# A two-layer decoder trunk on Trainium2: the residual kept transposed, the norm's root applied at eviction, expert down rows read four to a partition

## The chip, the cores and the metric

The kernel runs on one core of a Trainium2 chip. The metric is the time of the whole program on the device, in microseconds. PE is the matrix engine, DVE the vector engine, ACT the scalar engine, POOL the GpSimd engine, SP the queue that issues most of the transfers.

## What is computed

256 tokens of 1,024 features, float32 throughout, go through two layers and a last norm. Each layer adds a mixer and then a mixture of experts to the residual `h`:

```python
for layer in range(DEPTH):                       # DEPTH = 2
    hn = rms_norm(h, attn_norm_g[layer])         # x * rsqrt(mean(x^2) + eps) * gain
    if layer % 2 == 0: mix = mixer_ab(hn, ...)   # stick-breaking and retention heads
    else:              mix = mixer_c(hn, ...)    # windowed attention, with biases
    h = h + mix
    h = h + hierarchical_moe(rms_norm(h, ffn_norm_g[layer]), ...)
return rms_norm(h, final_norm_g)
```

The experts: 32 of them in 4 groups. A token takes the best group and the two best experts in it. An expert is `(silu(x @ w_gate[e]) * (x @ w_up[e])) @ w_down[e]`, with w_gate and w_up 1024x512 and w_down 512x1024. All weights of all experts are read once a layer: 32 x 3 matrices of 2.097 MB.

## The kernel before

**Weights.** A unit is one 2 MB block of weights, 16 KB on each partition. SP loads units into seven ring slots and four spare ones of the `arena` (the expert loop goes round over eight of these; three more, parked, hold down units of the first quad). A slot is reloaded when PE has counted up `used` for what was in it. Gate and up units are read as eight consecutive rows to a partition, one run of 16 KB; a down unit with `a (m p) n -> p (a m) n` (line 355), four rows of 4 KB that lie 128 rows apart.

**Residual and norms.** `h` lies with tokens on partitions, two blocks of 128. A norm (numbered 0 to 4: before mixer 0, experts 0, mixer 1, experts 1, and the last) does, for each block: ACT squares with a sum (`mean_squares`, 538), POOL adds eps and raises to -1/2 (`inverse_rms`, 473), DVE scales into `hr` (`norm`, 1138), PE turns eight tiles (`turn_normed`, 693), DVE evicts them times the gain into `hnT`, features on partitions (`spread_normed`, 1148). Only then can PE project (`project`, 717, and `in_proj`, 730).

**Mixer 0.** Seven input units; the first two go out transposed, products of 256 moving columns, the rest with 512 (lines 743 and 720). ACT evicts them (`evac`, 553). Heads are worked between the units. `out_proj` (846) takes token blocks as the stationary side and 512 weight columns as the moving one, in a low part (heads of the first kind) and a high part (second kind), and block 1's last products are broken by the turning of block 0's norm. `residual` (1244) adds two banks of a block to `h`.

**Experts** (PE 884, DVE 1259, ACT 600, POOL 486, SP 370). Router logits come out transposed from normed rows (`logits_of`, 703), go through ACT and are turned (`turn_logits`, 712). DVE chooses in some 20 small steps (1271 to 1293), PE ranks, DVE makes a 0/1 matrix `pick`. A quad is four experts with 32 token slots each. For quad i PE gathers its tokens (`gather`, 899: products of `hr` and `pick`), DVE evicts them times the gain (`take_rows`, 1334), `four` (907) does gate, up and down with four experts side by side, and `combine` (934) multiplies the output by the weighted pick into token rows, summed over all quads in four banks. After the first products of a quad have freed slots, SP issues the next loads, so that the transfers run ahead of PE. There are eight quads a layer.

**Mixer 1** adds its input bias at eviction (`add_bias`, 1392); POOL adds the output bias to `h` during the attention (521). `out_low` (1070) fills PE's waits between heads. After experts 1, the last norm is written block by block and sent out (453 to 457).

## Time and profile before

| | us |
|---|---|
| three runs: median, lowest, highest | 1250.41, 1247.34, 1256.53 |
| the profiled execution, and the span in it | 1254.63, 1252.8 |
| PE busy, DVE busy, ACT busy, POOL busy | 837.8, 174.4, 117.8, 44.2 |
| mean granted clock of PE, as a share of full | 0.832 |

The page cuts the span into 40 equal slices of 31.3 us and gives the share of each engine in tenths for each. The other views are the chain of work that ended last, the timeline of instructions, groups of instructions by line, and windows, which add up busy time, granted clock and transfer rate between two times. Times are microseconds from the span's start. "x128" counts instruction records; a float32 product has two of them. In brackets at the end of a timeline row stand the idle time before it and what ended it.

### The profile page before, as it was taken

To read this page: it belongs to the slowest core of one execution; us is meant where nothing else is said; L and a number is where in the kernel's file an instruction comes from. 1 tells how busy PE (TensorE), PEld (TensorE's weight loads), DVE (VectorE), ACT (ScalarE), POOL (GpSimd) and SP (SyncE) were. 2 spreads that over 40 slices of the span, in tenths; PEclk is the share of its full clock that TensorE was granted. 3 is DMA by queue.
4 is the path that set the end of the run, shared out by engine and by line. 5 is a ranking of instruction groups with operands and counts; after the bars stand their busy time and mean duration, and the time that the engine had idled before them with its cause. 6 is when DMAs were issued, how large, how long until landed. Compare 5 with 4: busy or idle time off the path is not lost.

```text
span 1252.8 us, 11735 instructions
## 1 busy us (share of the span) xinstructions
PE 837.8 (67%) x4938; PEld 382.0 (30%) x4938; DVE 174.4 (14%) x404; ACT 117.8 (9%) x237; POOL 44.2 (4%) x55
## 2 busy tenths in 40 slices
PE   6999978473737465565669898856473737465565
PEld 5655444131303121212224574512131303121211
DVE  1042432000000000000023543300000000000001
ACT  1145110000000000000010321000000000000001
POOL 0010100000000000000001300000000000000000
PEclk9999989787879696977779788887786879697868
DMA  9932744999999999999995435399999999999992
GB/s 368 385 135 96 275 195 195 422 417 428 418 424 423 423 422 421 429 418 428 416 403 213 177 135 201 134 428 419 429 416 424 422 423 421 423 427 420 426 417 120
DMA packets 66362, 439.00 MB, mean 350 GB/s; under 512 B 3601, under 2 KB 3601, under 8 KB 49809
## 3 DMA queue, kind: packets, MB, share of 16 engines
q1 hardware_dynamic: 65888, 435.97, 85.0%
q10 hardware_dynamic: 432, 2.43, 0.5%
q8 instruction: 32, 0.52, 0.2%
q14 instruction: 10, 0.07, 0.0%
HBM read 437.34 MB, written 1.05 MB: 350 GB/s over the span
## 4 chain that ended last, share of the span: by engine, by line
DMA 48%; PE 40%; SPq 6%; DVE 3%; issue 1%; ACT 1%; POOL 1%; POOLq 0%; DVEq 0%; ACTq 0%
PE bank L923 18%; DMA arena<-in_w_gate 17%; DMA arena<-in_w_down 15%; DMA arena<-in_w_up 14%; PE bank L720 9%; SPq L361 6%; PE bank L850 4%; PE bank L743 2%; PE bank L691 2%; DMA ring<-in_w_in_ab 1%; PE bank L903 1%; PE bank L708 1%; DVE h L1247 1%; PE bank L775 0%; PE bank L940 0%
## 5 line engine op out<-in xcount | busy, mean ns | idle before, releaser
L923 PE MATMUL bank<-ring,hnT 128*32 128x512 f32 x1792 | 283.6, 716 | 298.1 <-DMA ring<-in_w_up 82.0
L923 PEld LDWEIGHTS bank<-ring,hnT 128*32 128x32 f32 x1792 | 74.3, 129 | 486.1 <-issue 369.2
L923 PE MATMUL bank<-ring,arena 128*32 128x512 f32 x800 | 131.4, 683 | 61.0 <-DMA arena<-in_w_down 37.7
L923 PE MATMUL bank<-arena,hnT 128*32 128x512 f32 x256 | 142.9, 722 | 0.0
L720 PE MATMUL bank<-ring,hnT 128*128 128x512 f32 x256 | 114.4, 603 | 1.7 <-DVE hnT L1151 1.7
L1344 DVE TENSOR_TENSOR arena<-arena,bank 128x512 f32<-128x512 f32 x16 | 11.0, 688 | 565.8 <-PE bank L923 565.8
L923 PE MATMUL bank<-arena 128*32 128x512 f32 x224 | 78.8, 634 | 2.0 <-ACT arena L619 2.0
L923 PEld LDWEIGHTS bank<-ring,arena 128*32 128x32 f32 x800 | 36.6, 123 | 142.2 <-issue 123.5
L903 PE MATMUL bank<-arena,hr 128*128 128x128 f32 x512 | 65.5, 289 | 2.0 <-DVE arena L1311 2.0
L720 PEld LDWEIGHTS bank<-ring,hnT 128*128 128x128 f32 x256 | 48.4, 193 | 59.8 <-issue 56.9
L903 PEld LDWEIGHTS bank<-arena,hr 128*128 128x128 f32 x512 | 62.4, 203 | 14.0 <-issue 11.7
L940 PE MATMUL bank<-hnT,arena 128*128 128x512 f32 x128 | 57.7, 594 | 1.5 <-issue 1.5
L850 PE MATMUL bank<-ring,arena 128*128 128x512 f32 x128 | 57.8, 598 | 0.6 <-ACT arena L681 0.3
L619 ACT ACTIVATE arena<-bank 128x512 f32<-128x512 f32 x16 | 9.6, 597 | 339.3 <-PE bank L691 339.3
L490 POOL TENSOR_TENSOR arena<-arena,gate_all 128x256 f32<-128x256 f32 x16 | 9.9, 616 | 806.8 <-PE bank L691 772.6
L615 ACT ACTIVATE arena<-bank 128x512 f32<-128x512 f32 x16 | 9.6, 597 | 304.6 <-PE bank L923 304.6
L691 PE MATMUL bank<-early,arena 128*128 128x128 f32 x216 | 36.7, 301 | 2.2 <-DVE arena L1344 1.8
L1348 DVE COPY hnT<-bank 128x512 f32<-128x512 f32 x16 | 11.1, 691 | 178.2 <-PE bank L923 178.2
L691 PEld LDWEIGHTS bank<-early,arena 128*128 128x128 f32 x216 | 26.9, 153 | 25.6 <-issue 22.0
L923 PEld LDWEIGHTS bank<-arena,hnT 128*32 128x32 f32 x256 | 31.8, 129 | 9.6 <-issue 9.6
L850 PEld LDWEIGHTS bank<-ring,arena 128*128 128x128 f32 x128 | 23.3, 190 | 26.1 <-issue 26.1
L940 PEld LDWEIGHTS bank<-hnT,arena 128*128 128x128 f32 x128 | 23.1, 190 | 26.2 <-issue 26.2
(159 smaller groups left out, 532.2 us busy)
## 6 DMA issues: line engine op xcount, KB each, us to landing
ring<-in_w_gate SPq DMA_DIRECT2D x56, 2048.0 KB, 20.8
ring<-in_w_up SPq DMA_DIRECT2D x56, 2048.0 KB, 21.7
ring<-in_w_down SPq DMA_DIRECT2D x50, 2048.0 KB, 20.4
arena<-in_w_down SPq DMA_DIRECT2D x14, 2048.0 KB, 23.1
arena<-in_w_up SPq DMA_DIRECT2D x8, 2048.0 KB, 29.7
arena<-in_w_gate SPq DMA_DIRECT2D x8, 2048.0 KB, 28.9
ring<-in_w_in_ab SPq DMA_DIRECT2D x7, 2048.0 KB, 21.2
ring<-in_w_in_c SPq DMA_DIRECT2D x3, 2048.0 KB, 20.2
```

The lines of the kernel that those rows point to most:

```text
L361: sp.dma_start(view(j, LOOP_SLOTS[l][k]), expert_unit(l, e, j // QUAD)).then_inc(moe[l]["landed"][k], 16)
L691: return pe.transpose(dst, src, ident)
L708: op = pe.matmul(bank[2 * b][0:ROUTER, 0:P], router[:, l, k, :], hnT[:, k, b * P:(b + 1) * P], start=(k == 0), stop=(k == KD - 1))
L720: op = pe.matmul(dst[b][:], hnT[:, k, b * P:(b + 1) * P], unit[:, k, :], start=(k == 0), stop=(k == KD - 1))
L743: op = pe.matmul(dst[c // 2][:, (c % 2) * S:(c % 2 + 1) * S], slot_in(s)[:, k, c * P:(c + 1) * P], hnT[:, k, :], start=(k == 0), stop=(k = ...
L850: op = pe.matmul(bank[banks[2 * b + half]][:], t[:, c, b * P:(b + 1) * P], unit[:, c % 4, half * HALF:(half + 1) * HALF], start=(c == 0), ...
L903: op = pe.matmul(of_block(bank[4 + k // 4], k % 4), hr[:, b, k, :], pick[:, b, :], start=(b == 0), stop=(b == NB - 1))
L923: op = pe.matmul(dst[rows, :], lhsT[:, q, rows], unit[s][:, q, cols], start=(q == 0), stop=(q == steps - 1))
L940: op = pe.matmul(bank[2 * b + half][:], pick_wT[:, b * P:(b + 1) * P], e_y[:, half * HALF:(half + 1) * HALF], start=first, stop=last, skip ...
L1247: op = dve.tensor_tensor(h[:, b, cols], h[:, b, cols], bank[banks[2 * b + half]][:], ALU.add)
L1344: dve.tensor_tensor(e_h, e_h, bank[7][:], ALU.mult).then_inc(m["hidden"], 1)
L1348: dve.tensor_copy(e_y[:, 0:HALF], bank[4][:]).then_inc(m["y_low"], 1)
```

## The change

- The residual is `hT`, features on partitions, in eight chunks of 128 features (feature p*8+k in chunk k). The input comes transposed and the output leaves so; the host turns both and reorders the columns of the two output projections.
- Output projections and `combine` put out such chunks: weights or expert output are the stationary side, 256 tokens the moving one. DVE adds a chunk as soon as it is done, ACT multiplies it by the norm's gain into `hg` (`scale_chunk`) and squares it (`square_chunk`). DVE or POOL sum the squares of the chunks, PE sums over partitions, POOL takes the root.
- Projections work on `hg`, without the root. The root is put in at eviction: by ACT as a scale, in `add_bias`, in the rotary tables, or, for the two transposed units, as a row spread over the partitions by PE from a diagonal. Router logits stay without it (the choice doesn't change; the two exponentials take it as a scale).
- For the gather, PE turns 16 tiles of `hg` and ACT evicts them times the root (`tokens_out`). The rows of a quad carry the gain already; DVE and ACT evict one half each.
- Down units are read as four consecutive rows to a partition. PE turns the hidden rows with a step of four, and DVE and ACT evict the output with a step of eight.
- The output bias comes with the late table and is added in `residual`; the last gain is a column in the gain table. Their two row loads go. ACT issues its four table loads at once. The first weight unit and the input come in two halves each, alternating.

```diff
+hT = sb("hT", [P, KD, S])
+hg = sb("hg", [P, KD, S])
 hr = sb("hr", [P, NB, KD, P])
-hnT = sb("hnT", [P, KD, S])
+sq_sum = sb("sq_sum", [P, S])
+gains = sb("gains", [P, NORMS, KD])
...
-return w_down[l, one].rearrange("a (m p) n -> p (a m) n", p=P)
+return w_down[l, one].rearrange("a (p m) n -> p (a m) n", m=MH)
...
-for b in range(NB):
-    sp.dma_start(h[:, b, :], x_v[:, b, :]).then_inc(x_in[b], 16)
-for u in range(AB_UNITS):
+for j in range(2):
+    ks = slice(4 * j, 4 * j + 4)
+    sp.dma_start(hT[:, ks, :], xT[:, ks, :]).then_inc(x_in[j], 16)
+    sp.dma_start(slot_in(0)[:, ks, :], w_ab_v[:, ks, 0:HALF]).then_inc((first_half_in, w_landed[0])[j], 16)
+for u in range(1, AB_UNITS):
...
-last = experts(0, [(sinks_b[:], sinks, SWA_HEADS), (c_bin, b_in_c, C_IN * HALF), (c_bout, b_out_c, D)])
+last = experts(0, [(sinks_b[:], sinks, SWA_HEADS), (c_bin, b_in_c, C_IN * HALF)])
...
-experts(1, [(final_gain, final_norm_g, D)])
-for b in range(NB):
-    sp.wait_ge(out_ready, b + 1)
-    sp.dma_start(out_v[:, b, :], hr[:, b].rearrange("p k c -> p (k c)")).then_inc(out_done, 16)
-sp.wait_ge(out_done, 16 * NB)
+experts(1, [])
...
+    pool.wait_ge(ms_out, n + 1)
+    pool.tensor_tensor(rstd[:, n, :], ms[:, n, :], minus_half[:, 0:NB], ALU.pow).then_inc(rooted, 1)
+
+def sum_squares(n):
+    for k in range(1, KD):
+        pool.wait_ge(squares, KD * n + k + 1)
+        op = pool.tensor_tensor(sq_sum[:], sq_sum[:] if k > 1 else squared[:, 0, :], squared[:, k, :], ALU.add)
+        if k < KD - 1:
+            link(op)
+    op.then_inc(summed, 1)
...
+act.dma_start(gains[:].rearrange("p n k -> p (n k)"), gain_table).then_inc(gains_in, 16)
 act.dma_start(early[:], early_table).then_inc(early_in, 16)
...
+def scale_chunk(n, k):
+    act.activation(hg[:, k, :], hT[:, k, :], ACT.Copy, scale=gains[:, n, k:k + 1]).then_inc(scaled, 1)
+
+def square_chunk(n, k):
+    act.activation(squared[:, k, :], hT[:, k, :], ACT.Square, scale=D ** -0.5).then_inc(squares, 1)
+
+def wait_chunk(n, k):
+    act.wait_ge(h_done, KD * (n - 1) + k + 1)
+
+act.wait_ge(gains_in, 16)
+for k in range(KD):
+    if k % 4 == 0:
+        act.wait_ge(x_in[k // 4], 16)
+    scale_chunk(0, k)
+    if k % 4 == 3:
+        for j in range(k - 3, k + 1):
+            square_chunk(0, j)
+
+def tokens_out(l):
+
+    n = 2 * l + 1
+    act.wait_ge(ms_done, n + 1)
+    act.activation(ms[:, n, :], bank[OUT_BANKS[l][1]][:, SUMS:SUMS + NB], ACT.Copy,
+                   bias=EPS).then_inc(ms_out, 1)
+    act.wait_ge(rooted, n + 1)
+    for high in range(2):
+        for b in range(NB):
+            act.wait_ge(hr_turned, 4 * l + 2 * high + b + 1)
+            op = act.activation(flat(hr[:, b, 4 * high:4 * high + 4, :]), hr_bank(l, b, high)[:], ACT.Copy,
+                                scale=rstd[:, n, b:b + 1])
+    op.then_inc(hr_done, 1)
...
+for k in range(KD):
+    wait_chunk(2 * l + 1, k)
+    scale_chunk(2 * l + 1, k)
+    square_chunk(2 * l + 1, k)
+tokens_out(l)
...
-act.activation(e_y[:, HALF:D], bank[5][:], ACT.Copy).then_inc(m["y_high"], 1)
+act.activation(e_y[:, :, CAP * 2:P], by_partition(bank[5]), ACT.Copy).then_inc(m["y_high"], 1)
...
+def take_high(i):
+    act.wait_ge(m["gathered"], i + 1)
+    act.activation(flat(xeT[:, 4:8, :]), bank[5][:], ACT.Copy).then_inc(m["xe_high"], 1)
...
+for k in range(KD):
+    if u == 0 and k == 4:
+        mean_squares(0, bank[4])
+        pe.wait_ge(w_landed[s], 16)
+    if u == 0:
+        pe.wait_ge(scaled, k + 1)
+    for c in range(4):
         op = pe.matmul(dst[c // 2][:, (c % 2) * S:(c % 2 + 1) * S],
-                       slot_in(s)[:, k, c * P:(c + 1) * P], hnT[:, k, :],
-                       start=(k == 0), stop=(k == KD - 1))
+                       slot_in(s)[:, k, c * P:(c + 1) * P], hg[:, k, :],
+                       start=(k == 0 and c % 2 == 0), stop=(k == KD - 1), skip_group_check=True)
...
+def out_proj(l, t, unit, part, steps=range(32), order=range(KD)):
     for step in steps:
-        half, c = step // 4, 4 * part + step % 4
-        op = pe.matmul(bank[banks[2 * b + half]][:], t[:, c, b * P:(b + 1) * P],
-                       unit[:, c % 4, half * HALF:(half + 1) * HALF], start=(c == 0), stop=(c == KD - 1))
+        k, c = order[step // 4], step % 4
+        op = pe.matmul(chunk_of(OUT_BANKS[l], k), unit[:, c, k * P:(k + 1) * P], t[:, 4 * part + c, :],
+                       start=(part == 0 and c == 0 and k < 4), stop=(part == 1 and c == 3),
+                       skip_group_check=True)
     return op
+
+def logits_of(l, k):
+    pe.wait_ge(scaled, KD * (2 * l + 1) + k + 1)
+    if k == 0:
+        pe.wait_ge(late_in, 16)
+    for b in range(NB):
+        lo = b * LOGIT_PITCH
+        op = pe.matmul(bank[FREE_BANKS[l][0]][:, lo:lo + ROUTER], hg[:, k, b * P:(b + 1) * P],
+                       router[:, l, k, :], start=(k == 0 and b == 0), stop=(k == KD - 1),
+                       skip_group_check=True)
+    if k == KD - 1:
+        op.then_inc(moe[l]["logits"], 1)
+
+def turn_rows(l, high):
+    for b in range(NB):
+        for k in range(4):
+            op = turn(of_block(hr_bank(l, b, high), k), hg[:, 4 * high + k, b * P:(b + 1) * P])
+        op.then_inc(hr_turned, 1)
+
+def out_proj_high(l, t, unit, done):
+    for k in range(KD):
+        if k >= 4:
+            pe.wait_ge(h_done, KD * 2 * l + k - 3)
+        op = out_proj(l, t, unit, 1, range(4 * k, 4 * k + 4))
+        op.then_inc(done, 1)
+        if k > 0:
+            logits_of(l, k - 1)
+    logits_of(l, KD - 1)
+    turn_rows(l, 0)
+    mean_squares(2 * l + 1, bank[OUT_BANKS[l][1]])
+    turn_rows(l, 1)
...
+out_proj(0, catT, slot_out(0), 0, range(2 * pair, 2 * pair + 2))
...
+out_proj(0, catT, slot_out(0), 0, range(8, 28))
 for b in range(NB):
     pe.wait_ge(ab["gn"], b + 1)
     for c in range(4):
         op = turn(of_block(bank[2 + b], c), r_c[:, b, c * P:(c + 1) * P])
     op.then_inc(ab["gn_turned"], 1)
+out_proj(0, catT, slot_out(0), 0, range(28, 32)).then_inc(ab["used"], 1)
 pe.wait_ge(w_landed[(AB_IN + 1) % RING], 32)
-pe.wait_ge(ab["gn_cat"], 1)
-out_proj(catT, OUT_BANKS, 0, slot_out(1), 1).then_inc(ab["out"], 1)
 pe.wait_ge(ab["gn_cat"], 2)
-out_proj(catT, OUT_BANKS, 1, slot_out(1), 1, range(0, 6))
-turn_normed(1, 0)
-out_proj(catT, OUT_BANKS, 1, slot_out(1), 1, range(6, 8)).then_inc(ab["used"], 1)
+out_proj_high(0, catT, slot_out(1), ab["out"])
...
-for half in range(2):
-    for b in range(NB):
-        op = pe.matmul(bank[2 * b + half][:], pick_wT[:, b * P:(b + 1) * P],
-                       e_y[:, half * HALF:(half + 1) * HALF], start=first, stop=last,
-                       skip_group_check=True)
-        if last and half:
-            op.then_inc(m["combined"], 1)
+for k in range(KD):
+    if last and k >= 4:
+        pe.wait_ge(h_done, KD * (2 * l + 1) + k - 3)
+    op = pe.matmul(chunk_of(Y_BANKS, k), e_y[:, k, :], pick_wT, start=first and k < 4,
+                   stop=last, skip_group_check=True)
+    if last:
+        op.then_inc(m["combined"], 1)
...
-op = turn(of_block(bank[6], mh), e_h[:, mh * P:(mh + 1) * P])
+op = turn(of_block(bank[6], mh), e_h.rearrange("t (p m) -> t m p", m=MH)[:, mh, :])
...
+for step in range(NB * KD):
+    if step < KD:
+        pe.wait_ge(scaled, KD * 2 + step + 1)
+    if step == KD:
+        mean_squares(2, bank[5])
+    op = project([bank[j] for j in C_IN_BANKS[0]], slot_in(c_slot(0)), range(step, step + 1))
...
-pe.wait_ge(cc["att_low"], 1)
-out_low(0, 2)
 turn_low(1)
 turn_p(7)
-out_low(2, 5)
+pe.wait_ge(cc["att_low"], 2)
+out_low(0, 8)
 swa_values(6)
-out_low(5, 8)
+out_low(8, 16)
 swa_values(7)
-out_proj(attT, C_OUT_BANKS, 1, slot_out(c_slot(3)), 0).then_inc(cc["used"], 1)
+out_low(16, 32).then_inc(cc["used"], 1)
...
+mean_squares(4, bank[4])
+spread_rms(4, bank[5])
...
+for u, dst, by in ((0, sb_qT, over_rms_q), (1, sb_kT, over_rms)):
+    dve.wait_ge(ab["used"], u + 1)
+    for j in range(2):
+        op = dve.tensor_tensor(dst[:, 2 * j:2 * j + 2, :], bank[2 * u + j][:].rearrange("p (c n) -> p c n", c=2),
+                               by.unsqueeze(1).broadcast_to([P, 2, S]), ALU.mult)
+    op.then_inc(ab["qk_evac"], 1)
...
+def residual(k, banks, bias=False):
+    if bias:
+        op = dve.scalar_tensor_tensor(out=hT[:, k, :], in0=chunk_of(banks, k), scalar=out_bias[:, k:k + 1],
+                                      in1=hT[:, k, :], op0=ALU.add, op1=ALU.add)
+    else:
+        op = dve.tensor_tensor(hT[:, k, :], hT[:, k, :], chunk_of(banks, k), ALU.add)
     op.then_inc(h_done, 1)
-dve.wait_ge(ab["out"], 1)
-residual(0, OUT_BANKS)
-norm(1, 0)
-spread_normed(1, 0)
-dve.wait_ge(ab["used"], AB_UNITS)
-residual(1, OUT_BANKS)
-norm(1, 1)
-spread_normed(1, 1)
+def mixer_out(l, done):
+    for k in range(KD):
+        dve.wait_ge(done, k + 1)
+        residual(k, OUT_BANKS[l], bias=l == 1)
...
+mean_out(4, bank[4])
+rms_diagonal(4)
+dve.wait_ge(spread_done, 2)
+dve.wait_ge(scaled, NORMS * KD)
+by = bank[5][:, 0:S].unsqueeze(1).broadcast_to([P, 2, S])
+for j in range(KD // 2):
+    ks = slice(2 * j, 2 * j + 2)
+    dve.tensor_tensor(outT[:, ks, :], hg[:, ks, :], by, ALU.mult).then_inc(out_ready, 1)
```

## Rows read from the trace of the kernel before

**Rows 1.** The page, slices of 31.3 us: transfers in tenths, rate, and all packets.

```profile
DMA  9932744999999999999995435399999999999992
GB/s 368 385 135 96 275 195 195 422 417 428 418 424 423 423 422 421 429 418 428 416 403 213 177 135 201 134 428 419 429 416 424 422 423 421 423 427 420 426 417 120
DMA packets 66362, 439.00 MB, mean 350 GB/s; under 512 B 3601, under 2 KB 3601, under 8 KB 49809
```

**Rows 2.** The chain that ended last, in order of time: start, duration, what.

```profile
14.80 29.61 PE bank L743 x128
44.41 13.73 PE bank L720 x32
...
325.84 29.50 DMA arena<-in_w_gate
...
370.66 24.34 DMA arena<-in_w_down
```

**Rows 3.** Windows: length; busy (records) of PE, PEld, DVE, ACT, POOL; clock, DMA share, GB/s.

```profile
335.00:365.00 30.00, 18.16 (x130) 5.05 (x130) 1.12 (x2) 1.20 (x3) 0.61 (x1) 0.77 1.00 428
372.00:388.00 16.00, 13.05 (x95) 5.82 (x96) 0.69 (x1) 0.00 (x0) 0.00 (x0) 0.75 1.02 407
171.00:183.00 12.00, 8.08 (x43) 6.33 (x42) 3.98 (x5) 1.88 (x5) 0.79 (x2) 0.72 0.48 175
700.00:731.00 31.00, 27.43 (x135) 21.72 (x134) 20.39 (x65) 10.88 (x47) 9.06 (x4) 0.63 0.37 136
```

**Rows 4.** Timeline of the start: start, duration, engine, line, operation, tiles.

```profile
5.49 1.06 ACT L545 ACTIVATE hr<-h 128x1024 f32<-128x1024 f32 x1 [3.04 <-DMA h<-in_x]
```

**Rows 5.** Timeline, from mixer 0 to experts 0.

```profile
171.22 1.28 DVE L1247 TENSOR_TENSOR h<-h,bank 128x512 f32<-128x512 f32 x2 [0.87 <-PE bank L850]
...
183.09 0.17 DVE L1271 TENSOR_REDUCE tmp<-bank 128x2 f32<-128x8 f32 x1 [4.34 <-PE bank L714]
...
189.33 5.30 PE L903 MATMUL bank<-arena,hr 128*128 128x128 f32 x32 [1.00 <-DVE arena L1311]
...
196.01 7.07 PE L923 MATMUL bank<-ring,hnT 128*32 128x512 f32 x64 [1.27 <-DVE hnT L1337]
```

**Rows 6.** Timeline, from experts 0 to mixer 1.

```profile
642.47 3.67 PE L940 MATMUL bank<-hnT,arena 128*128 128x512 f32 x8 [0.76 <-issue]
...
652.97 8.93 PE L720 MATMUL bank<-ring,hnT 128*128 128x512 f32 x16 [0.78 <-DVE hnT L1151]
...
670.97 1.29 DVE L1397 TENSOR_TENSOR arena<-bank,arena 128x512 f32<-128x512 f32 x2 [7.21 <-PE bank L720]
```

**Rows 7.** Timeline, from mixer 1 to experts 1.

```profile
747.02 7.08 PE L850 MATMUL bank<-ring,arena 128*128 128x512 f32 x16
...
781.49 0.17 DVE L1271 TENSOR_REDUCE tmp<-bank 128x2 f32<-128x8 f32 x1 [4.40 <-PE bank L714]
...
787.72 6.42 PE L903 MATMUL bank<-arena,hr 128*128 128x128 f32 x32 [1.01 <-DVE arena L1311]
```

**Rows 8.** Timeline of the end.

```profile
1239.97 3.67 PE L940 MATMUL bank<-hnT,arena 128*128 128x512 f32 x8 [0.76 <-issue]
...
1248.42 1.28 DVE L1145 SCALAR_TENSOR_TENSOR hr<-h,rstd,arena 128x1024 f32<-128x1024 f32 x1 [0.77 <-POOL rstd L477]
```

**Rows 9.** Timeline inside experts 0, PE alone.

```profile
384.51 3.84 PE L903 MATMUL bank<-arena,hr 128*128 128x128 f32 x32
...
388.62 3.60 PE L940 MATMUL bank<-hnT,arena 128*128 128x512 f32 x8
```

**Rows 10.** Groups by line: form, count, busy and mean of one, idle time before.

```profile
L1141 DVE TENSOR_SCALAR hr<-h,rstd 128x1024 f32<-128x1024 f32 x8 | 10.7, 1333 | 18.1 <-POOL rstd L477 18.1
...
L490 POOL TENSOR_TENSOR arena<-arena,gate_all 128x256 f32<-128x256 f32 x16 | 9.9, 616 | 806.8 <-PE bank L691 772.6 <-DVE gate_all L1331 34.2
...
L627 ACT ACTIVATE arena<-bank 128x256 f32<-128x256 f32 x16 | 6.1, 378 | 6.1 <-PE bank L691 6.1
...
L1416 DVE TENSOR_TENSOR arena<-arena 128x256 f32<-128x256 f32 x4 | 1.4, 418 | 0.0
```

411 lines of the change are left out of this document (207 added, 204 removed).

## The prediction

> **What bounds the kernel now.** I read the page first, its slices and packets [rows 1]. Two long plateaus, the 8th to the 21st slice and the 27th to the 39th, have the DMA engines at 9 tenths and 403 to 429 GB/s: these are the two expert stages. Between them stand the mixers, with DMA at 2 to 7 tenths in the slices that they fill. So the kernel has two regimes. In an expert stage the end is set by bytes over rate; in a mixer, and in the hand-offs at its two ends, by the chain through PE and the small engines.
>
> The chain in order of time confirms it [rows 2]. The fourth load of a group of gates, issued at 325.84, lands 29.50 us later; that is the whole wait for the group. Four units of 2.097 MB at 428 GB/s are 19.6 us, so 9.9 us of older loads were still queued: PE may be that late before the DMA engines run dry. The windows show the rate [rows 3]: 428 GB/s while gate and up units land, 407 while down units land. The DMA share is full in both, so the difference is in how long the engines take for the same bytes.
>
> The same view has the first projection, and PE at full clock in it [rows 2]. Then I read the timeline at each hand-off: the start [rows 4], mixer 0 to experts 0 [rows 5], experts 0 to mixer 1 [rows 6], mixer 1 to experts 1 [rows 7], the end [rows 8]. There PE stands while squares, root, norm, 16 transposes and their evictions follow one another. From the last output product of mixer 0 (the next add starts at 171.22) to the first gate product at 196.01 are 24.8 us, in which DMA does little.
>
> **Prices.** A PE record (a product is two) is one pass. With 256 moving columns 128 records take 29.61 us, 0.231 each; with 512, 32 take 13.73 us, 0.429 [rows 2]. The gather's 32 records of 128 columns take 3.84 us inside a stage, 0.12 each [rows 9]; records with fewer columns I price the same. An ACT step of 128x256 is 0.38 us, a DVE step of 128x256 0.42, POOL's 0.62 [rows 10]; ACT's eviction of 128x512 is 0.60. For a hop between engines I put 0.07 us, a guess; a few hundredths more or less move no part by half a microsecond.
>
> **1. The start.** Before, PE's first projection starts at 14.80, released by the whole first unit [rows 2]. After, it needs the first half of x and of that unit. But ACT's queue no longer waits for the squares: early, late and decay tables (2.4 MB) are issued at once, ahead of the second x half in time. x had landed for the first square at 5.49 [rows 4]; the half unit (1.05 MB) plus the late table (0.5 MB) at 385 GB/s are 4.1 us more, so PE starts near 9.5 and its 64 records take 7.4, cold perhaps 9. The second half of x (0.5 MB) shares with decay (1.57 MB), 5.4 us, to about 14.5; then PE's sum of squares, placed ahead of k = 4, waits for 4 scalings, 4 squares and an add, 3.5 us, to 18.1. The remaining unit half lands near then too. Then 7.4 + 14.8 us and the spread of the root (1 us) end at 41.5 where 44.41 stood [rows 2]. I take 2.5 gained, with 0 (the tables take all of it) and 6 (no sharing) as bounds. Eviction of the first two units goes from ACT to DVE, with 7 adds, 2 copies and 4 table products; between 15 and 45 us DVE does nothing before, and PE's third unit covers it (14 us).
>
> **2. Mixer 0 to experts.** The output product is turned round: 64 products of 256 columns for 32 of 512, 128 x 0.231 = 29.6 us for 64 x 0.429 = 27.5, so 2 us more. Before, the last one ends at 171.2 [rows 5]. After, the high part can't start before both group norm blocks are turned; chunk 7 of the low part (1.85 us) covers this, so it starts near 157.7. Eight chunks of 1.85 us and seven logits of 4 records x 0.12 = 0.48 us give 18.2: the last chunk ends at 175.9. Behind it: add 0.42, scaling 0.38, logits 0.48, hops 0.2, together 1.4: the router starts at 177.3, where DVE's first router step stood at 183.09 [rows 5]. All other chunks' adds, scalings and squares lie under PE's 2.3 us a chunk, POOL's adds too (0.62). From there to the gather 6.24 us as before, to 183.5. In parallel runs what now feeds the gather: last square and POOL's add (1.9 us after the last chunk), 16 turned tiles and PE's sum of squares (to 3.8), ACT's copy, the root (0.57), ACT's four evictions of 0.6: 7.3 us after the chunk, 183.2. It just fits, so any slip there costs one for one. The gather took 5.30 us here and 3.84 inside the stage [rows 5, 9]; PE now idles less before it. The rows' eviction is split between DVE and ACT: 0.7 for 1.3. First gate product at 188.2 to 189.7 for 196.01: I take 7.0, bounds 3 and 9.
>
> A rule of the Trainium skill speaks against the warm gather: "TensorE: Matmul & The Clock Gate", section "Part 4: PE-mode transpose", says transposes don't count as PE work for the clock. Here the stretch 171 to 183, with turned rows in it, has a granted clock of 0.72 [rows 3]; no row shows whether they kept it low. By that rule both gathers stay cold and the sum is 3 us smaller.
>
> **3. The expert stages.** A down unit is now one run of 16 KB a partition, where it was four of 4 KB: 64 x 512 = 32,768 of the 49,809 packets under 8 KB are down's [rows 1]. It becomes the shape of a gate unit exactly, so I give it a gate unit's rate: 2.097 MB at 407 GB/s is 5.15 us, at 428 4.90, 0.25 less; a stretch in between would narrow it, so 0.24. 29 down units land in a saturated stage (the first quad's fourth and 28 more): 7.0 us. Bounds: 0 (the rate isn't from the run length) and 8. Each stage also read one row of 1,024 floats (output bias, final gain) to all 128 partitions, 0.5 MB, which now comes with a table or as 40 numbers a partition: 1.2 us each. So 8.1 a stage, 16.2 in all. PE's own work barely changes (combine: 16 records of 0.231 for 8 of 0.429, +0.3); DVE gives ACT half of the rows' eviction. In the quad shown combine ends at 392.2 and the down units land at 395.0 [rows 2, 9].
>
> **4. Experts 0 to mixer 1.** Before, combine starts at 642.47, the first projection at 652.97, and its bias is added at 670.97 [rows 6]. After, the 8 combine products take 3.7 us; adds (0.42) and scalings (0.38) follow at PE's 0.46 a chunk, and the waits from chunk 4 on are met. PE goes on at 646.2 with scaled chunks, 32 x 0.429 = 13.7 and 0.5 for the sum of squares: 660.5. Squares, adds and root are done about 8 us after the combine's start. Its weights landed long before. Saved 10.4, bounds 8 and 11.5.
>
> **5. Mixer 1 to experts 1.** The low output products now wait for both turned halves and have twice the records: their end at 754.1 [rows 7] becomes 755.9. The high part waits for both evictions, near 757.5. 18.2 us and 1.4 give the router at 777.1 for 781.49 [rows 7]; the gather, 6.42 us here, is 3.84 warm; the eviction saves 0.6. 5.0 to 7.6, I take 6.3.
>
> **6. The end.** Combine starts at 1239.97, the last scaling at 1248.42, span end 1252.8 [rows 8]: 12.8 us. After: ACT has 16 steps of 128x256 instead of two of 1.06 us: at 0.33 each (their starts overlap) 5.3 from 1.0 on, so 6.4; last add, PE's sum, mean, root, two diagonals and PE's spread 2.7; four DVE products of 0.69, 2.7; output DMA and the end as before, 3.1. 14.9: 2.1 lost, bounds 0 and 4.
>
> **Sum.** 2.5 + 7.0 + 16.2 + 10.4 + 6.3 - 2.1 = 40.3 us. The profiled execution took 1254.6 (span 1252.8), 4.2 above the median of the runs, 1250.4. I subtract from the median: 1210.
>
> **Strided reads.** Down's new row order makes PE turn the hidden rows with a step of four elements, and both copies of a quad's output read PSUM with a step of eight. No row shows either, for PE or for PSUM. In SBUF a step costs nothing: the norm that writes permuted took 1.33 us, the last, contiguous one 1.28 [rows 8, 10]. I take nothing. "SBUF — State Buffer" of the Trainium skill, section "Door 1: The DMA port swizzle", says that PSUM is read in lines of 8 bytes and steps beyond them cost; were the copies twice as long, only the last of each stage shows, 1.2 us in all.
>
> **Rivals.** (a) Down units keep 407 GB/s, because their rate comes from something else than the run length (their place in SBUF, PE's reads meanwhile). For it: the three kinds are loaded in turn, never alone. Against it: same bytes, same slots, same queue. Time 1210 + 14 = 1224. (b) The hand-offs give little: the sums of squares sit in PE's queue and ACT's evictions come after the root, so the gather waits in both layers. With 7 us of slip each, parts 2 and 5 are gone: 1210 + 13 = 1223; with a start that gains nothing, 1226. (c) The clock of mixer 1: 31 us at 0.63 [rows 3] shift in time; at full clock at most 31 x 0.37 = 11 us less, and about 8 with DVE and ACT on the same chain, or as much more if the next stretch falls too: 1202 to 1218. (d) Slower than before: the strided reads make a quad's turn, combine and copies so long that PE falls behind. It has 2.8 us until the down units land, and 9.9 us queued behind: 12.7 us a quad before DMA idles. It decides from there; to lose 1% net of the gains it takes 3.8 us more a quad over 14 quads, 16.5 us for work that takes about 6 now. Four times as long on all of it gives 18: 1210 + 14 x 5.3 = 1284. (e) The change does less than it says: the run length does nothing and hand-offs slip, 1240.
>
> **How the numbers follow.** My forecast with the clock's variation (c): 0.66. (a) 0.14, (b) 0.11, (e) 0.04, (d) 0.03, other 0.02. Range: 1199 (bounds of parts 1, 2, 5 and a warm mixer 1 together) to 1226, which takes in (a) and (b). One per cent, 12.5 us, is about what a measurement can tell from no change: faster by over 1% holds for all but (e) and (d): 0.93; within 1% 0.04; slower 0.03.
>
> **What would show it.** Down windows at 428 GB/s (part 3); packets under 8 KB down by some 32,768 and packets in all by 24,576; first projection at 9 to 10 with a wait at its middle; 18 us for the high part of each output projection, and 12 to 14 from its end to the first gate product; no idle of PE between combine and projection; 15 us from the last combine on. It is wrong if a quad's period doesn't fall by about 1 us, or if PE waits at the gather for ACT.

## The result, and the profile after

The change made the kernel faster: 1220.2 us median of four runs (1218.1 to 1226.0) beside 1249.2 for four of the kernel before (1247.3 to 1256.5). The ratio is 0.977, 95% interval 0.974 to 0.980. The prediction was 1210 with a range of 1199 to 1226. The profiled execution took 1218.1 us, its span is 1216.3.

The profiled pair differs by 36.5 us, the medians by 29.0. The runs of one kernel spread over 8 to 13 us; the stage table below shows where the profiles of one kernel differ. I cut the timeline of each run at the same events, the start of each: the start ends at the first projection with 512 columns, mixer 0 ends at the first gate product, experts 0 at the last combine, the hand-off at mixer 1's first projection, mixer 1 at the next first gate product, experts 1 at its last combine.

| kernel | span | start | mixer 0 | experts 0 | hand-off | mixer 1 (clock) | experts 1 | end |
|---|---|---|---|---|---|---|---|---|
| before | 1252.8 | 44.2 | 151.8 | 446.5 | 10.5 | 142.5 (0.84) | 444.5 | 12.8 |
| before, second profile | 1246.9 | 43.2 | 151.7 | 446.6 | 10.5 | 136.8 (0.90) | 445.3 | 12.8 |
| after | 1216.3 | 45.0 | 146.2 | 443.4 | 3.5 | 122.6 (0.97) | 438.1 | 17.5 |
| after, second profile | 1216.8 | 45.4 | 146.2 | 443.5 | 3.5 | 122.6 (0.97) | 438.1 | 17.5 |
| after, third profile | 1220.9 | 45.6 | 146.2 | 443.6 | 3.5 | 126.3 (0.93) | 438.2 | 17.5 |

All stages of one kernel but mixer 1 repeat within 1.0 us. Mixer 1 doesn't, in either kernel, and its granted clock goes with it. That is the first thing to read from the table: a difference of one pair of profiles carries the clock of mixer 1, up to 6 us of it in one kernel.

The page after, in slices of 30.4 us (clock in tenths, GB/s, packets), beside [rows 1]:

```profile
PEclk9999998777878687868689999969787878777787
GB/s 355 387 134 137 229 246 191 429 406 429 426 428 428 427 428 428 428 429 427 427 402 330 199 143 204 299 428 427 429 425 428 428 428 426 428 431 427 427 426 46
DMA packets 41947, 437.98 MB, mean 360 GB/s; under 512 B 3760, under 2 KB 3760, under 8 KB 17200
```

Packets fell by 24,415 and those under 8 KB by 32,609. The plateaus of the expert stages are now flat at 425 to 431, but for a slice of 406 near the start of the first and one of 402 at its end; before, apart from their last slices, they went between 416 and 429 [rows 1].

The start, the chain in order of time (start, duration, what), for [rows 2]:

```profile
1.18 13.30 DMA ring<-in_w_in_ab
14.57 8.96 PE bank L815 x32
...
45.15 13.73 PE bank L785 x32
```

The first projection starts at 14.57, where it stood at 14.80. It now waits for half a unit and not for a whole one, and gains nothing by it.

PE from mixer 0 to experts 0, timeline (start, duration, engine, line, tiles, records, in brackets the idle before), for [rows 5], and windows over the same place (length, busy of PE, PEld, DVE, ACT, POOL, clock, DMA share, GB/s):

```profile
176.40 0.53 PE L935 MATMUL bank<-late,hg 128*128 128x36 f32 x4
...
184.53 5.92 PE L1003 MATMUL bank<-arena,hr 128*128 128x128 f32 x32 [1.01 <-DVE arena L1433]
...
191.23 1.06 PE L1023 MATMUL bank<-ring,hg 128*32 128x512 f32 x8 [0.67 <-DVE hg L1458]
...
178.00:181.00 3.00, 2.43 (x23) 2.19 (x22) 2.40 (x15) 0.65 (x2) 1.43 (x2) 1.00 0.79 322
181.00:184.50 3.50, 1.48 (x6) 1.34 (x6) 1.76 (x8) 3.47 (x7) 0.00 (x0) 0.66 0.59 253
184.50:190.50 6.00, 5.97 (x33) 5.73 (x33) 2.46 (x18) 0.64 (x5) 0.61 (x1) 0.63 0.01 3
```

The last chunk's products and the logits of the seventh chunk are through at 176.9, the router starts at 178.3, the gather at 184.53; it runs at 0.63 of the clock.

Experts 0 to mixer 1, for [rows 6], then the end, for [rows 8]:

```profile
634.59 3.69 PE L1041 MATMUL bank<-arena,hg 128*128 128x256 f32 x16 [0.76 <-issue]
...
638.12 7.03 PE L785 MATMUL bank<-ring,hg 128*128 128x512 f32 x16
...
644.99 0.50 PE L771 MATMUL bank<-ones,sq_sum 128*128 128x1 f32 x4
...
652.62 1.41 DVE L1514 SCALAR_TENSOR_TENSOR arena<-bank,rstd,arena 128x512 f32<-128x512 f32 x2 [6.85 <-PE bank L785]
...
1198.80 3.69 PE L1041 MATMUL bank<-arena,hg 128*128 128x256 f32 x16 [0.76 <-issue]
...
1204.92 0.40 ACT L581 ACTIVATE hr<-hT 128x256 f32<-128x256 f32 x1
...
1206.52 1.01 PE L771 MATMUL bank<-ones,sq_sum 128*128 128x1 f32 x4 [4.02 <-DVE sq_sum L1248]
...
1209.07 1.22 PE L778 MATMUL bank<-tmp,ones 128*128 128x128 f32 x4 [1.54 <-DVE tmp L1262]
1210.33 2.48 DVE L1603 TENSOR_TENSOR hr<-hg,bank 128x512 f32<-128x512 f32 x4 [1.31 <-PE bank L778]
```

PE goes from the last combine product straight into the projection, with the sum of squares (0.50 us) in its middle. From the combine's start to the first bias add are 18.0 us for 28.5 before. At the end, 5.0 us lie between the last square's end (1205.3) and the first product of the result with the root (1210.33).

### The profile page after: what moved, and what is told of

It is laid out like the page before. It is cut to its first block, busy times and chain, and to the rows that moved or that the text cites. A ratio compares the mean times of both kernels' runs of the same rounds, so it can differ in the third digit from the quotient of the medians.

```text
span 1216.3 us, 12390 instructions
## 1 busy us (share of the span) xinstructions
PE 818.4 (67%) x5186; PEld 419.4 (34%) x5186; DVE 160.5 (13%) x420; ACT 148.3 (12%) x319; POOL 41.7 (3%) x52
## 3 DMA queue, kind: packets, MB, share of 16 engines
HBM read 436.30 MB, written 1.05 MB: 360 GB/s over the span
## 4 chain that ended last, share of the span: by engine, by line
DMA 48%; PE 38%; issue 7%; DVE 3%; SPq 2%; ACT 1%; POOL 1%; POOLq 0%; DVEq 0%; ACTq 0%
PE bank L1023 17%; DMA arena<-in_w_down 10%; DMA arena<-in_w_gate 9%; PE bank L785 9%; DMA arena<-in_w_up 7%; DMA ring<-in_w_up 7%; DMA ring<-in_w_down 7%; DMA ring<-in_w_gate 7%; PE bank L924 4%; PE bank L815 2%; SPq L392 2%; PE bank L1003 1%; DMA ring<-in_w_in_ab 1%; PE bank L764 1%; PE bank L935 0%
## 5 line engine op out<-in xcount | busy, mean ns | idle before, releaser
L1023 PE MATMUL bank<-ring,hg 128*32 128x512 f32 x1792 | 285.2, 720 | 302.4 <-DMA arena<-in_w_gate 87.8
L1023 PEld LDWEIGHTS bank<-ring,hg 128*32 128x32 f32 x1792 | 74.6, 129 | 491.7 <-issue 377.6
L1023 PE MATMUL bank<-arena,hg 128*32 128x512 f32 x256 | 142.7, 721 | 0.0
L785 PE MATMUL bank<-ring,hg 128*128 128x512 f32 x256 | 112.4, 595 | 0.0
L785 PEld LDWEIGHTS bank<-ring,hg 128*128 128x128 f32 x256 | 47.9, 190 | 56.3 <-issue 55.3
L1003 PEld LDWEIGHTS bank<-arena,hr 128*128 128x128 f32 x512 | 62.1, 202 | 14.0 <-issue 11.7
L924 PE MATMUL bank<-arena,ring 128*128 128x256 f32 x256 | 61.1, 389 | 0.9 <-DVE arena L1593 0.9
L1041 PE MATMUL bank<-arena,hg 128*128 128x256 f32 x256 | 58.1, 380 | 1.5 <-issue 1.5
L1041 PEld LDWEIGHTS bank<-arena,hg 128*128 128x128 f32 x256 | 47.6, 191 | 9.0 <-issue 3.3
L924 PEld LDWEIGHTS bank<-arena,ring 128*128 128x128 f32 x256 | 47.4, 192 | 7.7 <-issue 1.9
L672 ACT ACTIVATE arena<-bank 128x512 f32<-128x512 f32 x16 | 9.6, 597 | 288.1 <-PE bank L1023 288.1
L1023 PEld LDWEIGHTS bank<-arena,hg 128*32 128x32 f32 x256 | 31.8, 130 | 9.6 <-issue 9.6
L680 ACT ACTIVATE hg<-bank 128x512 f32<-128x512 f32 x16 | 9.6, 597 | 209.5 <-PE bank L1023 209.5
```

Source lines behind the costliest of these rows:

```text
L672: act.activation(e_h, bank[6][:], ACT.Silu).then_inc(m["silu"], 1)
L680: act.activation(e_y[:, :, CAP * 2:P], by_partition(bank[5]), ACT.Copy).then_inc(m["y_high"], 1)
L785: op = pe.matmul(dst[b][:], hg[:, k, b * P:(b + 1) * P], unit[:, k, :], start=(k == 0), stop=(k == KD - 1))
L924: op = pe.matmul(chunk_of(OUT_BANKS[l], k), unit[:, c, k * P:(k + 1) * P], t[:, 4 * part + c, :], start=(part == 0 and c == 0 and k < 4), ...
L1003: op = pe.matmul(of_block(bank[4 + k // 4], k % 4), hr[:, b, k, :], pick[:, b, :], start=(b == 0), stop=(b == NB - 1))
L1023: op = pe.matmul(dst[rows, :], lhsT[:, q, rows], unit[s][:, q, cols], start=(q == 0), stop=(q == steps - 1))
```

## The experiments

The ratios are to runs of the kernel before on the same chip as each edit; the stages come from one profile each and are cut as above:

| kernel | median | ratio (95%) | start | mixer 0 | experts 0 | hand-off | mixer 1 (clock) | experts 1 | end |
|---|---|---|---|---|---|---|---|---|---|
| after | 1222.0 | 0.977 (0.973 to 0.981) | 45.4 | 146.2 | 443.5 | 3.5 | 122.6 (0.97) | 438.1 | 17.5 |
| after, third | 1223.9 | 0.978 (0.975 to 0.982) | 45.6 | 146.2 | 443.6 | 3.5 | 126.3 (0.93) | 438.2 | 17.5 |
| e1_down_4k | 1234.7 | 0.987 (0.983 to 0.990) | 46.3 | 143.8 | 450.1 | 3.5 | 126.2 (0.93) | 444.5 | 17.4 |
| e4_before_down_16k | 1244.9 | 0.992 (0.989 to 0.996) | 41.7 | 152.2 | 443.1 | 10.5 | 142.9 (0.84) | 440.0 | 12.8 |
| e6_rows_back | 1221.2 | 0.977 (0.974 to 0.980) | 44.7 | 145.2 | 443.9 | 3.5 | 122.6 (0.97) | 440.6 | 17.0 |
| e2_tables_late | 1217.1 | 0.973 (0.970 to 0.975) | 40.3 | 146.2 | 443.2 | 3.5 | 126.3 (0.93) | 438.1 | 17.5 |
| e3_end_on_pe | 1216.4 | 0.972 (0.969 to 0.975) | 45.5 | 146.2 | 443.4 | 3.5 | 126.3 (0.93) | 438.1 | 16.0 |
| e5_warm | 1215.2 | 0.970 (0.968 to 0.973) | 44.8 | 143.6 | 442.7 | 3.5 | 121.0 (0.99) | 438.8 | 17.3 |
| e7_sums_first | 1227.0 | 0.981 (0.979 to 0.984) | 44.9 | 143.6 | 442.9 | 9.9 | 123.6 (0.97) | 439.2 | 17.0 |
| e8_before_filled | 1250.2 | 0.998 (0.996 to 1.000) | 44.4 | 152.1 | 446.6 | 10.5 | 137.1 (0.91) | 445.5 | 12.8 |
| all_three | 1208.9 | 0.969 (0.966 to 0.971) | 39.7 | 143.5 | 442.8 | 3.5 | 120.9 (0.99) | 438.7 | 15.9 |

### Both kernels again, unedited

> The changed kernel unaltered, as the reference for the runs beside it and for a second profile of mixer 1. If the fast clock of its attention (0.94 to 1.00 between 684 and 712 us) belongs to the change, the stretch from the last combine of experts 0 to the first gate product of experts 1 takes 126 us again; if it was luck of one execution, it is 130 to 136 and the granted clock drops to about 0.6 for some 20 us, as in the kernel before.

> The changed kernel unedited, for comparison on the same chip with the two others: 1218 to 1224 us, ratio 0.974 to 0.98; mixer 1 at 122.6 or 126.2 us from its first projection to its first gate product, the two lengths seen in the profiles so far.

> The kernel before, unaltered, for a second profile. If the slow clock of its attention (0.50 between 710 and 731) is of the program's own making, mixer 1 from the last combine of experts 0 to the first gate product takes 153 us again; if it was luck, 143 to 147.

They came out at 0.977 and 0.978. From the last combine to the next first gate product the changed kernel takes 126.1 and 129.8 us, and the second profile of before 147.3 where the first has 153.0: the clock of the attention is in part the luck of an execution, in both kernels. The span of that second profile is 1246.9, 5.9 shorter than the first, 5.7 of it in mixer 1.

### The length of a run in the down units

In the changed kernel, the old view of the down weights with the turn that fits it; and the new view alone in the kernel before.

```diff
 # e1_down_4k: in the changed kernel
-w_down[l, one].rearrange("a (p m) n -> p (a m) n", m=MH)
+w_down[l, one].rearrange("a (m p) n -> p (a m) n", p=P)
-op = turn(of_block(bank[6], mh), e_h.rearrange("t (p m) -> t m p", m=MH)[:, mh, :])
+op = turn(of_block(bank[6], mh), e_h[:, mh * P:(mh + 1) * P])
 # e4_before_down_16k: the same two lines the other way round, in the kernel before
```

> The changed kernel with the down units read as before (four runs of 4 KB to a partition) and the hidden rows turned without a step; nothing else. Run length theory: the down windows fall back to about 407 to 410 GB/s and a quad to 59.6 us, so each expert stage is 4 us (0.58 a quad) to 7 us (my sum) longer, 8 to 14 in all. Rival, that the rate isn't from the run length: same time as the changed kernel.

> The kernel before with only the down units' rows changed: four consecutive rows to a partition, hidden rows turned with a step of four. Run length theory: 8 to 14 us faster than before, windows of down units at 428 GB/s, a quad at 59.0 instead of 59.6 us. Rival, that the stepped turn costs PE what the loads give: same time as before. Rival, no effect of the run length: same.

Undone it costs 12.7 us of median (1234.7 for 1222.0), 6.6 and 6.4 of it in the two expert stages; alone it gives 7.5 (1244.9 for 1252.4 on that chip; by the ratio 9.5), 3.4 and 4.5 to 5.3 in them, at the lower edge of the 8 to 14 expected. One window of 352 us in experts 0 shows it, for before, after, e1 and e4 in this order:

```profile
260.00:612.00 352.00, 197.80 (x1362) 74.22 (x1361) 17.77 (x29) 12.39 (x24) 3.70 (x6) 0.79 1.01 423
```

```profile
255.00:607.00 352.00, 200.06 (x1432) 84.71 (x1428) 14.55 (x23) 15.32 (x30) 3.69 (x6) 0.78 1.01 428
```

```profile
254.00:606.00 352.00, 201.59 (x1420) 84.75 (x1412) 14.55 (x23) 15.33 (x30) 3.69 (x6) 0.78 1.01 422
```

```profile
258.00:610.00 352.00, 199.79 (x1380) 75.62 (x1382) 17.98 (x29) 12.39 (x24) 3.69 (x6) 0.79 1.01 429
```

423 and 422 GB/s with runs of 4 KB, 428 and 429 with runs of 16 KB, the DMA share full in all. So the run length sets the rate; rival (a) falls. Over 352 us that is 352 x 5/428 = 4.1 us in before and 352 x 6/428 = 4.9 in e1. PE holds the strided turns and copies without falling behind, for the DMA engines never wait in it: rival (d) falls. Why e1 loses 2 to 3 us a stage more than e4 gains isn't settled: part of it lies outside this window.

### The row loads

```diff
+spot_at = spare(1) + C_IN * HALF + KV_HEADS * S
+sp.dma_start(arena[:, spot_at:spot_at + D], row_bcast(b_in_c, D)).then_inc(decay_in, 16)
```

> The changed kernel with one more row of 1,024 floats read to all 128 partitions in each expert stage, as the kernel before did (0.5 MB each). If such a row costs its bytes, 1.2 us a stage, 2.4 in all; if it lies in a gap that the queue has there anyway (the transfers fell to 216 GB/s for 3 us after the remaining row), 0 to 0.5.

With one row load of 0.5 MB back in each stage, experts 1 is 2.5 us longer and experts 0 0.4, where its bytes at 428 GB/s are 1.2 us. The other eight profiles with runs of 16 KB in the changed kernel have 438.1 to 439.2 in experts 1, so 440.6 stands out; but it is one profile, and the median doesn't move (ratio 0.977). In experts 0 another such load (the input bias) remains, and there the stream breaks in both (after, then e6):

```profile
239.00:255.00 16.00, 8.47 (x64) 2.46 (x64) 0.00 (x0) 0.00 (x0) 0.00 (x0) 0.68 0.91 385
```

```profile
238.00:254.00 16.00, 8.73 (x64) 2.56 (x64) 0.00 (x0) 0.00 (x0) 0.00 (x0) 0.68 0.93 392
```

385 and 392 GB/s, at a DMA share of 0.91 and 0.93: 16 us that lose 1.6 and 1.3. In these profiles a second row behind the first one costs next to nothing, the only one of a stage 2.5 us.

### The tables behind the squares

ACT's issues of late and decay table moved behind its loop over the first norm.

```diff
-act.dma_start(late[:], late_table).then_inc(late_in, 16)
-act.dma_start(flat(decay), decay_table).then_inc(decay_in, 16)
 for k in range(KD):
     ...
+act.dma_start(late[:], late_table).then_inc(late_in, 16)
+act.dma_start(flat(decay), decay_table).then_inc(decay_in, 16)
```

> The changed kernel, with the late and the decay table issued by ACT after the last square of the input instead of at once. If the tables' place in the queues is what kept the first half unit from landing before 14.5, PE starts at 7 to 9 us and the second unit ends 5 us earlier: 4 to 5.5 us faster. Rival, that the half unit's landing is set by something else (its own many short runs, the queue's start): PE starts at 12 or later and the gain is under 2 us.

Its chain in order of time:

```profile
1.18 8.33 DMA ring<-in_w_in_ab
9.60 9.29 PE bank L815 x32
```

The first projection starts at 9.60 for 14.57, and the start ends 5.1 us earlier (40.3 for 45.4); the median falls by 4.9. So the two tables, issued on a second queue beside SP's, hold up the half unit by 5 us. Only without them do the two halves gain anything: the start is then 3.9 us shorter than before.

### The end's sums on PE

```diff
 for k in range(KD):
     wait_chunk(4, k)
     square_chunk(4, k)
+for k in range(KD):
     scale_chunk(4, k)
...
-mean_squares(4, bank[4])
+for k in range(KD):
+    pe.wait_ge(squares, KD * 4 + k + 1)
+    for b in range(NB):
+        op = pe.matmul(bank[4][:, SUMS + b:SUMS + b + 1], squared[:, k, b * P:(b + 1) * P], ones[:, 0:1], ...)
+op.then_inc(ms_done, 1)
```

> The changed kernel; at the very end ACT squares all chunks before it scales any, and PE sums the squared chunks itself (16 small products in one bank) instead of DVE adding eight chunks first. If DVE's chain of adds (1202.9 to 1206.5) is what made the end long, the end falls from 17.5 us to 14 or 15, 2.5 to 3.5 us faster. Rival, PE's products on a cold clock are as slow as DVE's adds: within 1 us.

```profile
1204.21 3.44 ACT L581 ACTIVATE hr<-hT 128x256 f32<-128x256 f32 x8 [1.26 <-DVE hT L1377]
1206.37 3.76 PEld L1231 LDWEIGHTS bank<-ones,hr 128*128 128x128 f32 x32
1206.58 3.63 PE L1231 MATMUL bank<-ones,hr 128*128 128x1 f32 x32
...
1206.50:1210.30 3.80, 3.71 (x34) 3.60 (x32) 0.75 (x3) 3.77 (x10) 0.00 (x0) 1.00 0.02 4
```

ACT's squares end at 4.60 us behind the combine's start instead of 6.5, but PE's 32 records take 3.63 us, 0.11 each, and that at full clock (1.00 in the window). The end is 16.0 us for 17.5: the expected 2.5 to 3.5 us didn't come, and it wasn't the low clock of the rival that took them. The median fell by 5.6, more than the profile accounts for; runs with other clocks in mixer 1 can make that up, so I take the 1.5 as shown and not the rest.

### PE kept at work around the choice

Idle products into a bank that is free, behind the turned tiles (512 and 256 columns) and ahead of the first gather (512); `flat_hg` stands for `hg` with its chunks side by side.

```diff
+for cols in (4, 2):
+    pe.matmul(bank[6][:, 0:cols * P], ones[:], flat_hg[:, 0:cols * P], ...)
 pe.wait_ge(m["chosen"], 1)
...
+pe.matmul(bank[6][:], ones[:], flat_hg[:, 0:4 * P], ...)
 gather(0)
```

> The changed kernel with idle work for PE while DVE routes: two products of 512 and 256 columns behind the turned rows and one of 512 ahead of the first gather, written where nobody reads, in each layer. If the gather is slow (5.93 and 5.48 us for 3.84 inside a stage) because PE idled before it, the gathers take 3.8 to 4.2 us: up to 2 us a layer, 3 to 4 us faster. Rival, the gather's first records wait for something else (the root's rows, the one-hot matrix): gathers as slow as before, and the kernel 0 to 1 us slower.

```profile
179.20 1.07 PE L764 MATMUL bank<-early,hg 128*128 128x128 f32 x8
...
183.75 3.84 PE L1006 MATMUL bank<-arena,hr 128*128 128x128 f32 x32
...
180.00:183.70 3.70, 3.36 (x15) 1.65 (x13) 2.44 (x12) 3.31 (x5) 0.34 (x1) 1.00 0.82 350
183.70:187.60 3.90, 3.85 (x33) 3.65 (x33) 2.47 (x17) 1.25 (x5) 0.61 (x1) 1.00 0.02 4
```

The gather takes 3.84 us at full clock for 5.92, with the same 16 turned tiles ahead of it. From its start to the first gate product are 4.6 us in both layers. Mixer 0 is 2.6 us shorter and mixer 1 is 1.6, and the ratio is 0.970; but e1 has a mixer 0 of 143.8 us with a slow gather, so not all of the 2.6 is the gather's. All four gathers behind such fillers (here and in all_three) take 4.6 us to the gate. Of the 16 in the eight profiles of the changed kernel without fillers, 15 take 6.3 to 7.4, and one, in layer 0 of e7 below, has 4.6 unaided:

```profile
183.84 3.84 PE L1003 MATMUL bank<-arena,hr 128*128 128x128 f32 x32 [1.01 <-DVE arena L1432]
```

### PE's wait ahead of mixer 1, and the clock in it

In the changed kernel, the sum of squares moved ahead of the first projection. In the kernel before, two idle products put where PE waits in the attention (`flat_hnT` is `hnT` side by side).

```diff
 # e7_sums_first, in the changed kernel
+mean_squares(2, bank[5])
 for step in range(NB * KD):
-    if step == KD:
-        mean_squares(2, bank[5])
 # e8_before_filled, in the kernel before
 swa_values(0)
+for _ in range(2):
+    pe.matmul(bank[1][:], ones[:], flat_hnT[:, 0:4 * P], start=True, stop=True, ...)
 swa_scores(3)
```

> The changed kernel with one thing undone: PE's sum of squares for mixer 1's norm stands ahead of the first projection instead of in its middle, so PE waits for all squares and POOL's adds before it projects, as the kernel before waited for the whole norm. Theory (the 16 us from mixer 1's first bias add to its first gate, where I had counted 6, are mostly the granted clock, and the clock of mixer 1 hangs on how PE's idle stretches fall): stage from the last combine to the first projection 3.5 to about 8.5 us, and mixer 1 itself as long as in the changed kernel or longer by up to 4 us, by whichever clock it is granted; 3 to 5 us slower in all if the clock stays, up to 9 if it falls back toward that of the kernel before. Rival (the 10 us are work that the change removed, not clock): hand-off 5 us longer, mixer 1 exactly 122.6 or 126.2 us as before, 5 us slower in all.

> The kernel before with one edit: two idle products of 512 columns (1.7 us) into an unused bank between the first values and the fourth pair of scores in mixer 1, where PE stands idle for 2.31 us (706.2 to 708.5 in the profile) behind DVE's roping of the second half of q. Nothing is taken off any chain. In the profile of before PE goes from 2.4 to 1.2 GHz right behind that idle stretch and stays there for some 23 us; in four runs of the changed kernel and its relatives the same idle stretch, 2.32 us, is followed by 0 to 9 us at 1.2 GHz. Theory (the 10 us by which mixer 1 beat my sum are clock, and the fall is due to that idle stretch): the fall at 708 is gone, mixer 1 takes 127 to 133 us instead of 136.8 to 142.5, and the kernel is 5 to 12 us faster than before, 1238 to 1245, by an edit that only adds work. Rival (the clock falls there for the load or the time since the expert stage, not for the idle): the granted clock still falls near 708, and the time stays within 2 us of 1250.

In e7 the hand-off is 6.4 us longer, mixer 1 is 123.6 us at 0.97, between the two lengths of the changed kernel; the median is 3 to 5 us above it. A wait ahead of mixer 1 doesn't bring back the low clock of before. It doesn't tell the theory from its rival either, since both allowed this length.

Where that low clock starts shows in PE's timeline and the windows around it. Before, with a window of its second profile as the last line:

```profile
708.49 0.80 PE L1032 MATMUL bank<-arena 64*128 64x128 f32 x4 [2.31 <-DVE arena L1432]
...
684.00:706.00 22.00, 21.77 (x92) 11.20 (x90) 11.55 (x28) 6.19 (x20) 4.80 (x3) 1.00 0.35 117
709.00:732.00 23.00, 21.73 (x107) 18.52 (x103) 13.35 (x46) 8.89 (x39) 4.71 (x2) 0.51 0.29 108
...
706.50:722.50 16.00, 13.83 (x74) 11.76 (x75) 10.42 (x34) 6.77 (x27) 6.11 (x3) 0.57 0.51 195
```

After, then its third profile:

```profile
690.34 0.52 PE L1136 MATMUL bank<-arena 64*128 64x128 f32 x4 [2.32 <-DVE arena L1550]
...
690.00:694.00 4.00, 3.66 (x20) 3.01 (x20) 3.87 (x14) 2.45 (x13) 0.00 (x0) 0.58 0.72 240
694.00:712.00 18.00, 15.99 (x135) 13.36 (x135) 13.22 (x52) 10.71 (x44) 0.00 (x0) 1.00 0.47 177
```

```profile
691.50:703.00 11.50, 10.23 (x57) 8.85 (x54) 5.81 (x23) 5.28 (x22) 0.00 (x0) 0.55 0.58 217
```

And e7, then e8:

```profile
695.50 0.49 PE L1135 MATMUL bank<-arena 64*128 64x128 f32 x4 [2.32 <-DVE arena L1549]
...
695.50:703.50 8.00, 6.14 (x55) 5.22 (x55) 5.75 (x21) 4.57 (x20) 0.00 (x0) 1.00 0.77 297
```

```profile
706.68 1.94 PE L1088 MATMUL bank<-hnT,ones 128*128 128x512 f32 x4
709.15 0.49 PE L1032 MATMUL bank<-arena 64*128 64x128 f32 x4 [0.54 <-DVE arena L1435]
...
715.93 0.80 PE L1032 MATMUL bank<-arena,hnT 64*128 64x128 f32 x4 [2.63 <-ACT hnT L650]
...
706.00:714.00 8.00, 6.76 (x46) 4.70 (x45) 7.93 (x21) 3.01 (x13) 8.00 (x4) 1.00 0.64 243
716.00:724.00 8.00, 8.00 (x39) 6.58 (x40) 4.31 (x19) 1.86 (x8) 0.00 (x0) 0.50 0.42 171
```

In each kernel PE is at full clock, stands idle for 2.3 us behind DVE's roping of the second half of q, and then may drop to 1.2 GHz (0.5): for some 23 us in before and 14 in its second profile, 3.5 and 10 in two profiles of after, not at all in e7. (These lengths are worked out from the windows: 11.5 us at a mean of 0.55 are 10.4 at 0.5 and the rest at full.) In e8 the two products (1.94 us) cover that idle time and the fall at 708 is gone. But the turned q now makes PE wait 2.63 us for ACT at 713, and the clock falls there for some 10 us. So my expectation missed: the fall hangs on an idle stretch, but closing the one lets the next do it. Mixer 1 is 137.1 us, as in the second profile of before, and the median is 1250.2 for 1251.1. What did change is the spread: 12 runs lie within 3.3 us, where 17 of before on that chip spread over 9.6.

### Three edits together

> The changed kernel with three edits together: the late and decay tables issued behind the first squares, the end's sums of squares taken on PE with ACT's squares ahead of its scalings, and PE kept at work with idle products ahead of the gather of each layer. If the gains add up, in the profiled span 4.9 for the start, 1.5 for the end and 2.5 plus 1.6 at the gathers are 10.5 us, so a span near 1206 and a median near 1209 beside 1221 of the changed kernel. If a rise of the clock in one place is paid back in another (the rival), it is no faster than the one with idle products alone, 1215.

The late tables, the end's sums on PE and the idle products at the gathers add up: the span of 1205.1 is 15.8 below that of the changed kernel on the same chip, 5.9 in the start, 2.7 in mixer 0, 5.3 in mixer 1, 1.6 in the end. That is more than the 10.5 expected, because mixer 1 of that profile of the changed kernel was 3.7 us longer than in its two others; beside the second profile the difference is 11.7. 1208.9 us is the lowest median of all kernels, 3.1% below the kernel before.

## Why the prediction was right, and where its sum was off

The sign and the range held, and so did the mechanisms of the hand-offs and of the run length. The start and the warm gather did not come, and two terms were mis-sized. The sum was 40.3 us; the medians differ by 29.0. By the profiled pair, with the clock of mixer 1 taken apart:

| step | predicted | profiled pair |
|---|---|---|
| 1, start | +2.5 | -0.8 |
| 2, mixer 0 to its first gate | +7.0 | +5.6 |
| 3, experts 0 | +8.1 | +3.1 |
| 4 and 5, last combine to first gate of experts 1 | +16.7 | +26.9, of which clock 7 to 10 |
| 3, experts 1 | +8.1 | +6.4 |
| 6, end | -2.1 | -4.7 |
| sum | 40.3 | 36.5, without the clock 27 to 30 |

**Clock, rival (c).** Before, 23 us of mixer 1 at 0.51 lose 23 x 0.49 = 11.3 us of full clock; after, 4 us at 0.58 lose 1.7; that is 9.6 less. What such a loss costs in time the unedited pairs show. The third profile of after loses 11.5 x 0.45 = 5.2, 3.5 more than the first, and takes 2.6 us longer from mixer 1's first projection to its high output products (94.8 for 92.2). The second of before loses 16 x 0.43 = 6.9, 4.4 less than the first, and is 4.5 us shorter there (97.8 for 102.4). By that the 9.6 are worth 7 to 10 us of the 26.9, an estimate, and the other 17 to 20 stand beside 16.7.

Without the clock the pair differs by 27 to 30 us, and the medians by 29.0. So it is the luck of its clock that the profiled pair, at 36.5, lies closer to the sum than the medians. I had put the clock in as a scatter around the sum with no sign; it was a gain in every pair of profiles, since PE's idle stretches were followed by shorter falls. I know no reason for that which a run shows. What the sum had too much, the steps outside mixer 1 show: 3.3 us in the start, 1.4 in step 2, 6.7 in the two expert stages, 2.6 in the end.

**Step 1 failed.** "The half unit (1.05 MB) plus the late table (0.5 MB) at 385 GB/s are 4.1 us more, so PE starts near 9.5": it started at 14.57, and at 9.60 with the tables out of the way. I had let the decay table fall on the second half of x only. (The "64 records" of the half unit are 32; the 7.4 us were right for 32 at full clock, and the trace has 8.96.) The bound of 0 had this case ("the tables take all of it"); I had chosen against it. The rest of step 1 held: e2's start of 40.3 is 3.9 better than before.

**Step 2 held but for its last term.** By the plan the last chunk would end at 175.9, the router start at 177.3, the gather at 183.5; mixer 0 began 0.7 later, and they came at 176.9, 178.3 and 184.5. The gather then took 5.92 us and the first gate product came 6.70 behind its start, where I had allowed 4.7 to 6.2 with a warmer clock. The reason given ("PE now idles less before it") was true and not enough. PE stood for 1.61 and 1.01 us ahead of the gather, where it had stood for 3.86 and 1.00:

```profile
186.84 0.63 PE L894 MATMUL bank<-tmp,early 128*128 128x32 f32 x2 [3.86 <-DVE tmp L1293]
```

Yet the clock fell there, to 0.66 in the 3.5 us ahead of it, and the gather was longer than before (5.92 us for 5.30). Rival (b), ACT's evictions after the root, didn't come: the gather waited 1.01 us for DVE's `pick`, the router's own chain.

The Trainium skill's "TensorE: Matmul & The Clock Gate", section "Part 4: PE-mode transpose", came out with the right number, cold gathers in both layers. That the tiles keep the clock low the traces don't bear out: it was 1.00 in the window 178 to 181 that holds the 16 turned tiles, and in e7 the gather behind the same tiles and the same idle time ran at full clock. With the idle time filled (e5) it did so in both layers. But the fillers are products, so no run here says whether the tiles count for less than products would; what the runs show is that filling the idle time was enough.

**Step 3, the size.** The mechanism held: flat at 428, 16 KB runs the cause. The term of 7.0 us a stage was mis-sized. I took 407 GB/s from a window of 16 us [rows 3] and gave it to 29 units; the mean over 352 us of before is 423, which is 4.1 us in that window. That makes 0.17 us a down unit for my 0.24 and some 5 us for the 29; the edits had 3.4 to 6.6 a stage. Down units pass through the queue among gates and ups, so a trough of 407 is followed by stretches above 428. A quad's period in experts 0 (mean of the last four, from gathered rows to gathered rows) fell from 59.6 to 59.0 us, 0.6 where I had said "about 1 us" as the test: by that test the step stands in doubt, and it was the test that took the trough for the mean. The row load's term, 1.2, was 0.4 in one stage and 2.5 in the other (e6); it cost more than its bytes, and the row that is left in experts 0 already pays for it.

**Steps 4 and 5 held.** 3.5 us from the last combine to the first projection (3.7 said), bias add 10.5 earlier (10.4 said), and the rest as above. In step 5 two misses cancel: from the high part's start to the gather were 24.1 us for 25.8, as a logits product of 36 columns took 0.37 us for 0.48, and from the gather to the first gate product 6.25 for 4.6, as that gather stayed cold too (5.47 us). e7 prices the first of them: with PE waiting for the squares the hand-off is 9.9 us.

**Step 6, the size.** ACT's sixteen steps ended as said (the last square 6.5 us behind the combine for 6.4). "Last add, PE's sum, mean, root, two diagonals and PE's spread 2.7" took 5.0: PE's two small groups were 1.01 and 1.22 us at the low clock (0.50), where I had put them at full, and the adds ended 1.1 us behind the last square for 0.4. Add 0.16, 0.69 and 0.48 for mean, root and diagonals, and six hops of some 0.05, and the 5.0 is there; the hops were as guessed.

**Strided reads.** I had taken nothing, against "Door 1: The DMA port swizzle" of "SBUF — State Buffer" in the Trainium skill. The groups by line of after (count, busy us, mean ns, idle before) hold both kinds of eviction of 128x512:

```profile
L1458 DVE COPY hg<-bank 128x512 f32<-128x512 f32 x16 | 11.1, 692 | 48.6 <-PE bank L1003 48.6
L1467 DVE COPY hg<-bank 128x512 f32<-128x512 f32 x16 | 11.1, 692 | 170.0 <-PE bank L1023 170.0
...
L672 ACT ACTIVATE arena<-bank 128x512 f32<-128x512 f32 x16 | 9.6, 597 | 288.1 <-PE bank L1023 288.1
L680 ACT ACTIVATE hg<-bank 128x512 f32<-128x512 f32 x16 | 9.6, 597 | 209.5 <-PE bank L1023 209.5
```

L1467 and L680 are the copies that read PSUM with a step of eight, L1458 and L672 read the same size in one piece: 692 ns and 692 on DVE, 597 and 597 on ACT. What that page prices is matmuls with such an access pattern to PSUM; for these copies, with a step of eight floats, the rows show no price.

## What to carry to other kernels

Take the rate of one kind of load from a mean over a whole period of the loop, never from the window in which it is slowest, and put the test in the same unit. A first load that must be early should have the transfers to itself: here 2 MB of tables on another queue took back the whole gain of splitting it. And before crediting work with a change in an engine's stage, lay the granted clock of both kernels side by side in short windows: here about a third of the largest gain was clock.

## What the runs showed of the hardware

- The same idle stretch of PE (2.31 to 2.32 us, in the same place of the attention) was followed by some 23, 14, 10, 3.5 and 0 us at 1.2 GHz in five profiles. What decides between them stays open.
- A filler of 1.94 us in the one idle stretch moved the fall to the next one, some 7 us later, and left the median at 1250.2 for 1251.1. Fillers around the gathers, the last idle time of their stages, brought each of them to 3.84 us, from gather to gate 1.6 to 2.8 us less than in the 15 slow cases.
- One row of 4 KB read to 128 partitions, alone in a stage of 2 MB loads, cost 2.5 us for 0.5 MB in the one profile that has it, twice its share of the bytes; in the 16 us around such a load the rate was 385 GB/s for 428.
- Units of 2 MB in runs of 4 KB a partition, one in three, kept the mean at 422 to 423 GB/s for 428 to 429.
